# Fifty-seven matmuls of constants on TensorE, in five places where it stood idle

## The reference, cut to what matters

```python
def reference(x, c, ..., final_norm_w_2):
    x = first_block(x, c, ada_w, ..., w_ffn_out)
    return second_block(x, positions_2, attn_norm_w_2, w_in_2, ...)

def first_block(...):
    mod = silu(c) @ ada_w + ada_b                     # six vectors sh, sc, ga
    h = rmsnorm(x, pre_mix_g) * (1.0 + sc1) + sh1
    y = hybrid_mixer(h, w_in, ...)                    # GLU, causal conv, stick-breaking attention
    x = x + ga1 * rmsnorm(y, post_mix_g)
    h = rmsnorm(x, pre_ffn_g) * (1.0 + sc2) + sh2
    x = x + ga2 * rmsnorm(swiglu_ffn(h, ...), post_ffn_g)

def second_block(...):
    proj = rms_norm(x, attn_norm_w) @ w_in            # r_q, r_k, r_v, r_g, c_q, c_kv, k_pe
    y_ret = retention_group(r_q, r_k, r_v, r_g, positions, ret_gn_w)
    y_mla = mla_group(c_q, c_kv, k_pe, positions, ...)  # latent attention, 8 heads
    x = x + concat([y_ret, y_mla]) @ w_out
    x = x + conv_ffn(rms_norm(x, ffn_norm_w), w_up, conv_w, conv_b, w_down)
    return rms_norm(x, final_norm_w)
```

## Time and profile before

| what | value |
|---|---|
| median of 3 runs | 1443.74 us |
| lowest and highest of the 3 | 1442.77 and 1447.46 us |
| span of the profiled execution | 1443.1 us |
| mean granted clock of TensorE in it, as a share of full speed | 0.977 |
| TensorE busy (PE) | 1364.2 us, 95% of the span |
| VectorE busy | 872.9 us, 60% |
| ScalarE busy | 638.8 us, 44% |

### The profile page before, as it was taken

How to read it: one execution, slowest core, us unless ns; L and a number is a source line. 1 busy time by engine, 2 the same in 40 slices (tenths; PEclk the granted TensorE clock), 3 DMA queues, 4 the chain that set the end, 5 groups by cost and what they waited for, 6 DMA issues and landing times. The chain is left out here.

```text
span 1443.1 us, 16364 instructions
## 1 busy us (share of the span) xinstructions
PE 1364.2 (95%) x6216; PEld 1115.5 (77%) x6216; DVE 872.9 (60%) x1057; ACT 638.8 (44%) x782; POOL 90.5 (6%) x67
## 2 busy tenths in 40 slices
PE   6999999989889999999997999879999999999997
PEld 3789888767558888888885788658778888888885
DVE  5799888657764423333335648777657745763663
ACT  4324777654354223222223755568546423432332
POOL 0000000011100092000010000000020000000001
PEclk9999999989999999999998999999999999999999
DMA  9534111136523432232221251130222232223222
GB/s 379 193 133 132 59 58 44 36 140 235 231 74 131 139 115 88 87 117 88 80 102 59 88 132 59 45 81 1 67 109 88 87 117 88 87 90 114 87 67 78
DMA packets 27590, 151.69 MB, mean 105 GB/s; under 512 B 3281, under 2 KB 3793, under 8 KB 14609
## 3 DMA queue, kind: packets, MB, share of 16 engines
q1 hardware_dynamic: 27536, 150.97, 30.1%
HBM read 143.88 MB, written 2.10 MB: 101 GB/s over the span
## 5 line engine op out<-in xcount | busy, mean ns | idle before, releaser
L1406 DVE TENSOR_TENSOR w_lo<-raw,w_hi 128x2048 fp32r<-128x2048 f32 (+2 forms) x114 | 251.4, 2205 | 128.2 <-ACT w_hi L862 124.5
L862 ACT ACTIVATE w_hi<-raw 128x2048 fp32r<-128x2048 f32 (+2 forms) x109 | 196.6, 1804 | 116.1 <-PE psum L506 80.6
L506 PE MATMUL psum<-h_hi,w_hi 128*128 128x512 f32 x712 | 181.6, 395 | 2.5 <-DVE w_lo L1406 2.3
L506 PE MATMUL psum<-h_hi,w_lo 128*128 128x512 f32 x712 | 178.9, 391 | 0.0
L506 PE MATMUL psum<-h_lo,w_hi 128*128 128x512 f32 x712 | 177.6, 390 | 0.0
L506 PEld LDWEIGHTS psum<-h_hi,w_hi 128*128 128x128 f32 x712 | 133.7, 190 | 32.0 <-DVE w_lo L1406 3.6
L506 PEld LDWEIGHTS psum<-h_lo,w_hi 128*128 128x128 f32 x712 | 134.1, 188 | 27.9
L506 PEld LDWEIGHTS psum<-h_hi,w_lo 128*128 128x128 f32 x712 | 133.7, 189 | 27.8
L1705 DVE TENSOR_TENSOR act_p<-act_a,psum 128x512 f32<-128x512 f32 x22 | 15.1, 687 | 112.4 <-PE psum L506 112.4
L506 PE MATMUL psum<-xg_hi,w_hi 128*128 128x512 f32 x336 | 83.0, 389 | 0.0
L506 PE MATMUL psum<-xg_lo,w_hi 128*128 128x512 f32 x336 | 83.0, 389 | 0.0
(11 more groups left out here) (344 smaller groups left out, 2201.2 us busy)
## 6 DMA issues: line engine op xcount, KB each, us to landing
raw<-w_ffn_in SPq DMA_DIRECT2D x22, 1024.0 KB, 4.7
raw<-w_up SPq DMA_DIRECT2D x22, 1024.0 KB, 4.8
ada_first<-ada SPq DMA_DIRECT2D x16, 512.0 KB, 11.3
raw<-w_gate SPq DMA_DIRECT2D x8, 1024.0 KB, 4.8
raw<-w_mix_out SPq DMA_DIRECT2D x8, 1024.0 KB, 4.9
raw<-w_ffn_out SPq DMA_DIRECT2D x8, 1024.0 KB, 4.8
raw<-w_down SPq DMA_DIRECT2D x8, 1024.0 KB, 4.7
ada_mid<-ada SPq DMA_DIRECT2D x11, 512.0 KB, 6.1
```

The source lines that it names most:

```text
L506: last = mm(ps, w[slot][:, k, t * P:(t + 1) * P], part(xv, k0 + k), start=first, stop=final)
L862: A(w_hi[slot][:, 0:stage.kc, :], raw[slot][:, 0:stage.kc, :], ACT.Copy).then_inc(sem["w_hi_done"], 1)
L1406: return tt(out_lo, full, high.bitcast(F32), ALU.subtract)
```

## The change

Matmuls whose result nobody reads are put into TensorE's order at the five places: 22 of `ones` by `ones` (128 columns, fp32) at A, and 8, 8, 9 and 10 of `ident_r` by four of the constant matrices (512 columns, fp32r) at C, B, D and E. Each writes a bank that is overwritten later by a matmul that starts anew. No other engine's program, no semaphore and no wait is changed.

```diff
+            four_consts = rounded[:, 0:4, :].rearrange("p a n -> p (a n)")
+
+            def keep_busy(into, n):
+
+                for _ in range(n):
+                    mm(into, ident_r, four_consts, start=True, stop=True)
+
             pe.wait_ge(sem["in_ones"], 16)
             stat_chunks("pre_mix")
+            for _ in range(22):
+                mm(bank[0][:, 0:P], ones[:, :], ones[:, :], start=True, stop=True)
...
                 if n == 4:
                     pe.wait_ge(sem["group_free"], st["latent"].g0 + 2)
+                    keep_busy(bank[3], 8)
                     for c in range(2):
                         pe.wait_ge(sem["c_sq"], c + 1)
...
                     n = 2 * i + s
+                    if n == 0:
+                        keep_busy(bank[4], 8)
                     if s == 0:
                         pe.wait_ge(sem["qk_hi"], 4 * (PAIRS + i) + 4)
...
             up_query(2)
             up_query(3)
+            keep_busy(bank[4], 9)
             up_wait(up_release(st, 0))
             group_var(bank[0], 2, sq_up)
...
             for n in range(HEADS):
+                if n == 0:
+                    keep_busy(bank[3], 10)
                 mla_transpose(n)
```

## The result

| | before | after |
|---|---|---|
| median | 1443.70 us (1440.54 to 1449.71, 8 runs) | 1436.56 us (1431.95 to 1439.01, 8 runs) |
| ratio, 95% interval | | 0.9942, 0.9923 to 0.996 |
| span of the profiled execution | 1443.1 us | 1436.7 us |
| granted clock in it | 0.977 | 0.985 |

The account below looks back on a forecast made before the run. TensorE, busy 95% of the span, bounds the kernel; half-clock work behind five idle stretches can be won. C, B and D 3.5, A 0.5, E 0.4 sum to 4.4 us: 1443.7 - 4.4 = 1439.3, 8-in-10 range 1436.8 to 1443.3.

Parts of the forecast that it names:

- A: Start of the first projection, half clock from 22.10 to 28.70 us: gain 0.5 us, bounds 0 and 0.6.
- C: Latent attention, head 0, from scores at 861.07 to values at 869.47 us: gain 1.6 us, bounds 1.0 and 1.7.
- B: From the sum of squares at 905.62 to the second values matmul at 910.20 us: gain 1.7, bounds 1.4 and 1.8.
- D: Four matmul records between 951.00 and 953.77 us, ahead of up_query(4): gain 1.05 us, bounds 0.7 and 1.3.
- E: Transposes and scores of head 1, half clock from 974.40 to 981.00 us: gain 0.4 us, bounds 0 and 1.7.
- the sum of 3.5: Gain in us at C, B and D together: (1.6 + 1.7 + 1.05) x 0.8.
- 4 in 5: Chance, in another execution, that the clock falls behind an idle stretch of 2.0 to 3.1 us; applied to C, B, D.
- the fifth stretch of the prediction: Idle stretch of 2.12 us ahead of 965.55, followed by work at full clock; the other four were followed by half clock.
- all of it: Rival, chance 0.13: clock usually falls before at every place, never after, E included; gain 6.5 us, 1437.2.
- not held: Rival, chance 0.18: constant matmuls don't count as work, or gains at C and D are hidden; 0 to 1 us, 1443.2.
- slower: Rival, chance 0.05: added matmuls run at half clock and end late at C, B, D and E; 5 us lost, 1448.7.
- E gives nothing: Rival, chance 0.14: transposes don't hold the clock between 973.7 and 977.56 us, so the 0.4 is lost; 1439.7.

Follow-up runs that it names:

- 2: Only the 22 matmuls at A added to the kernel before: median 1443.09 us, ratio 0.9981.
- run 3: Only the ten matmuls at E added to the kernel before: median 1441.05 us, ratio 0.9978.
- 8: The change plus matmuls of constants in the second idle stretch of E and in seven more stretches: median 1432.47 us, ratio 0.9927 to before.
- 12: The kernel of 8 plus 8 fillers at the attention start and 10 behind the first feed-forward group: median 1430.49 us, ratio 0.9914 to before.
- run 13: The whole change with the 22 matmuls at A over 8 columns in place of 128: median 1435.55 us, ratio 0.9937 to before.
- 1: Only the added matmuls at C, B and D put into the kernel before: median 1440.88 us, ratio 0.9981.
- 6: The change without the 22 matmuls at A: median 1440.34 us, ratio 0.9969 to before.
- run 9: The change without A, with 8 fillers in the first attention head's wait for t_lo: median 1438.20 us, ratio 0.9969 to before.
- run 14: The whole change with A as 6 matmuls of 512 columns in place of 22 of 128: median 1437.63 us, ratio 0.9945 to before.

## Why the prediction was right and wrong

**Fit and clock, right; the sum of 3.5 with some luck.** The fillers fit as computed, constants hold the clock at C, B and D, and no wait behind them takes the gain back. By the ledger, C is 8.33 on average where untreated (before, 2, 3) and 6.81 with the filler, 1.5; B 6.69 and 6.07, 0.6; D 8.69 and 7.13, 1.6. Sum 3.7, times 3.8 (0.9), forecast 3.5. The forecast had 1.3, 1.4 and 0.8 for them, so B came out lower and D higher, and the errors cancel. B is a matter of how often the clock falls: untreated, C and D fell in three traces of three, B in one. D's size was misread: from 951.00 to 953.77 only three matmul records are spent in full, the fourth starts 0.07 us ahead of the end, and the same distance at full clock is 1.39 and not 4 x 0.43. With E's four of four the falls are 11 of 13, where I took 4 in 5. Idle stretches of about 2 us are the unsure ones: B, with 2.04, fell in one trace of three, and the fifth stretch of the prediction, 2.1 us ahead of the first latent scores and filled in runs 8 and 12 alone, in five of the other fourteen; where it fell, that cost 0.2 us or less.

The Trainium skill, TensorE: Matmul & The Clock Gate (Part 1), says that the number of slow matmuls differs from run to run; by that rule a discount belongs in the sum. These traces agree: behind much the same wait at A (5.5 and 5.3 us), 14 matmuls started at half clock in the trace of before and 8 in that of run 3.

**The term "E 0.4", mis-sized.** The step "So the clock is likely to fall all the same, a little later, over the same scores" failed. The idle stretch of 1.69 us came, but only in the first trace of after was the work behind it at half clock. E gives 2.0 in its own stretch, the value of the rival "all of it" (1.6) or a little over, and 2 to 3 by times. The prediction reasoned that an idle stretch of 1.7 us behind transposes, with 0.8 us ahead of them, would bring the clock down; it did in one trace of nine (in six of them with the 0.8 us ahead, in three with none). This is the term that failed most plainly: 0.4 against 2.0.

**The term "A 0.5", and "The added matmuls have no cost elsewhere".** Where A stands the forecast is right: 0.54 between the two traces, and zero in the traces in which the fall is shorter. But by times A is worth 2.2 to 3.0 us (standard errors 0.8 to 0.9), and that is not the clock at A: in run 13 it fell and the time was as low as with the change. What fits is the number of instructions.

Over all 16 traces: the ten with 22 matmuls at A have the attention start at 20.29 to 21.40 (mean 20.5); of the five without A, before has 20.30, runs 1, 3 and 6 have 22.42, 23.53 and 25.33 (22.9 for the four), and run 9, filled there, 22.11. That is 2.4 us.

With the 22 matmuls the records of the queue 8 (kind "instruction") come about 9 us earlier from the start on: 31.5 to 32.1 in place of 40.6 to 42.2, and 115.2 to 116.2 in place of 123.0 to 125.2. With six matmuls they are at 39.6 and 124.1. In nine of the ten that record falls beside the issue of the `key_dup` transfers, which then takes 3.0 to 3.2 us; in the tenth (after) it comes at 116.17, just behind, and the issue takes 1.17 as in all the others. The issue of `w_gate` starts at 118 and not at 116 (but ends only half a microsecond later), and the transfer of `qkT` at 122, which it would share the DMA engines with, is in time: `pair` starts at 128.5 to 131.5, against 132.3 to 133.4 in four of five. That the later load is what frees the transfer isn't shown: no experiment moves that load alone, one trace without A (before) has an early transfer too (129.2), and so, nearly, has run 14 (131.2). Why A is worth 2 to 3 us stays open; what is shown is that it isn't the clock at A, that it moves the records, and that the attention start is the stretch in which the traces with and without A differ most.

So the profile that I worked from had the early transfer at the attention start, and an effect of A there could not be seen in it.

**"0.6 below the median", wrong.** A run's time is 1.8 above its span here (1438.5 and 1436.7 for after), so the profiled execution of before probably stood about a microsecond above its median. This changes nothing in the terms.

**The account.** C, B, D 3.7, E 2.0, A 0.2 in place (24.34 on average in the five traces without it) and 2.4 at the attention start, this last from a few single traces with a cause that is not shown: 8.3, against 8.3 (1.5) and 6.7 (0.9) measured. Of the rivals, "not held" and "slower" fell, and "E gives nothing" too: the transposes and the scores behind them ran at full clock. "All of it" had the size right for E; its total of 1437.2 is near the median, but it has neither A's size nor its place.

## What to carry to other kernels

Before pricing an edit on one trace, ask of every stretch whether another execution would show it the same; profile two or three kernels that differ elsewhere, and compare the distance between the same two instructions in each. Added instructions are not free of side effects, even if they signal nobody: they move the moments of the instruction records in the DMA queues, by 9 us here. Where TensorE idles for 2 to 3 us in front of work that is awaited, matmuls of constants were worth 0.6 to 2 us at each place here, provided they end before the awaited data; a filler about a microsecond too long cost 0 to 0.9 us.

## What was not expected of the hardware

- Time follows the clock from execution to execution of the same kernel. With the time at half clock taken as (1 - granted clock) x 2 x time, the 30 executions of before in one set have 58 us of it on average, and the time rises by 0.36 us for each (correlation 0.87); two more sets of 29 give 0.41 and 0.49, one of 11 gives 0.33, each within 0.04 to 0.08. The Trainium skill, TensorE: Matmul & The Clock Gate (Terms), puts the penalty at one half of the throttled time where the clock is halved; one of the sets agrees, the others lie below it. A likely reason, not tested apart, is that some of the half clock falls on idle time or on work that another engine hides: the last 4.6 us of the trace of before are at half clock, with no matmul in them.
- With every such stretch filled (run 12) the 6 executions lie between 1429.74 and 1431.19, where 29 of before in the same set lie between 1437.92 and 1447.45; the standard deviations are 0.6 and 2.4 us. The fillers also make the kernel steadier. The conv stretch alone varies from 48.4 to 53.1 us from trace to trace where nothing is filled in it.
- With a record of kind "instruction" beside it, a pair of DMA issues took 3.1 us in place of 1.17, in nine traces of sixteen; in the other seven the issue behind the pair took 2.0 in place of 0.6, so that the three together differ by only half a microsecond. Where the record comes depends on code far ahead: 22 matmuls more at 17 us, whatever their width (runs 2 and 13), move it by 9 us, 100 us later.
